# A fp32 two-model transformer forward in one kernel: where weight conversions, table loads and filler matmuls stand in each engine's order

## The chip, the cores and the metric

One core of one Trainium2 chip runs the whole program. The metric is the time of one execution in device microseconds. The engines named here are PE (TensorE, with its weight loads PEld), DVE (VectorE), ACT (ScalarE), POOL (GpSimd) and SP (SyncE, which issues the weight loads).

## The reference

256 tokens, width 1024, everything in fp32. Two models of two layers each follow one another:

```python
x = x + moba_attention(rms_norm(x, norm_mix[0]))        # 8 heads; one block: causal softmax
x = x + squared_relu_mlp(rms_norm(x, norm_mlp[0]))      # relu(x @ up)**2 @ down, 4096 wide
x = x + pool_mixer(rms_norm(x, norm_mix[1]))            # trailing means over 2, 4, 8, 16 tokens
x = x + squared_relu_mlp(rms_norm(x, norm_mlp[1]))
x = rms_norm(x, norm_final)
# second model; post norms on every branch
x = x + rms_norm(mla_mixer(rms_norm(x)))                # latents 384 + 256, 8 heads, rope part 64
x = x + rms_norm(swiglu(rms_norm(x)))                   # silu(h @ gate) * (h @ up) @ down, 2816 wide
k, v = rms_norm(x, kv_src_g) @ w_kv_shared              # 16 heads of 64
x = x + rms_norm(chunked_mixer(rms_norm(x), k, v))      # chunked attention, relative bias
x = x + rms_norm(swiglu(rms_norm(x)))
```

## The kernel before

**Split products.** Every fp32 product is made from three products of rounded parts: hi x hi, hi x lo and lo x hi. A weight is loaded in chunks of 128 x 2048 (1 MB; 176 chunks, four slots `raw`, `whi`, `wlo`). ACT rounds a chunk (`whi`, L669), DVE subtracts (`wlo`, L1082), PE takes it: three matmuls of up to 512 columns (L1916 to L1918), or a wide form with the activations' two parts side by side (L2015, L2018; at an entry tile by tile L2095, L2097). The chunk's slot is free for the next rounding once PE has used it (`w_used`), and free for the next load once DVE has subtracted (`lo_ready`). Activations are split the same way: ACT copies a turned tile out of PSUM (L725), DVE subtracts (L1209); for heads L747 and L1387; for hidden tiles L783 or L829 and L1419.

**Order.** Nothing schedules this program: each engine has a program written by hand, and semaphores tie them. `cursor` counts the chunks that ACT or DVE has converted; `hi_next` and `lo_next` convert the next one, `lo_before(c)` converts up to chunk c, `hi_half` and `lo_half` convert one half of 1024 columns at a time. An instruction that waits holds up all behind it on its engine. Chunks by stage: qkv 0 to 11, output 12 to 15, first MLP 16 to 47, pool 48, second MLP 49 to 80, latents (`wa`, `uqr`, `uq`, `ukv`) 81 to 89, output 90 to 93, first gated layer 94 to 126, shared keys and values (`kvk`, `kvv`) 127 to 134, queries 135 to 138, output 139 to 142, second gated layer 143 to 175.

**Entries of stages.** A post norm (`post_entry`, ACT's `split_stats`) takes the squares by halves of a tile, scales x + y (`xs`, L1255), and PE turns it (L1958) and starts the next layer while the norm's second factor is still open: `sum_entry`, `late_roots` and `ffn_layer` carry it as a diagonal (`probs`, L1169) that PE spreads over a row (L2107) and DVE multiplies into the gates. Two token tiles t = 0, 1 follow one another. In the latent preparation the 384 and 256 wide latents are normed, turned in four parts (`turn_lora`), and multiplied by `uq`, `uqr` and `ukv`. In an attention, heads (or pairs of heads in the second one, `pair_step`) are staggered: scores, exponentials, probabilities, values, output copies (`copy_out` on ACT, `split_out` on DVE), and weight conversions come between (`due`). `keep_busy` runs matmuls on constants whose result nobody reads. `preload(ACT.Sqrt)` makes a table load (L663) at a chosen place. The last norm is `post_stats` on ACT and `post` on DVE, whole tiles of 1024 columns at a time, and SP stores four halves.

## Time and profile before

| | us |
|---|---|
| median of three runs | 1115.6 |
| the runs | 1114.78, 1115.79, 1115.6 |
| the profiled execution | 1115.45 |
| its span in the trace | 1112.9 |
| PE busy in it | 1079.3 |
| first idle: the start, until the first weights and x are there | about 2.5 |
| last matmul's end to the span's end | about 8.3 |

The span is what the profiler saw from the first to the last instruction; the time of the execution holds 2.55 us more around it. In the timeline a row starts with its start in us from the span's start, then the busy time; in brackets stands the idle time before it on its engine and what ended that. Of the matmuls, ends are modelled, so the pause before one counts from a modelled end.

### The profile page before, as it was taken

What the parts mean: (1) busy time and instruction counts of PE and PEld (TensorE: products, weight loads), DVE (VectorE), ACT (ScalarE), POOL (GpSimd) and SP (SyncE); (2) the same over time, 40 slices, a digit from 0 to 9 for tenths busy, and PEclk for the clock granted to TensorE, in tenths of its full rate; (3) what the DMA queues carried; (4) which work ended last, traced back from release to release, by engine and by line L of the source; (5) the groups of instructions that cost most, each with busy time, mean ns of one, the idle gap of its engine ahead of it and who ended that gap; (6) DMA issues with size and microseconds to landing.
All of it is one profiled execution on the core that took longest, in us unless ns stands there. A gap on an engine that the chain in (4) does not pass through costs nothing.

```text
span 1112.9 us, 15305 instructions
## 1 busy us (share of the span) xinstructions
PE 1079.3 (97%) x5820; PEld 911.4 (82%) x5820; DVE 743.5 (67%) x1056; ACT 558.8 (50%) x710; POOL 37.2 (3%) x58
## 2 busy tenths in 40 slices
PE   8999999999999999999999999999999988999997
PEld 6887888888888888889778788888789677888885
DVE  5756665656777565668677776565897867766665
ACT  5556444444454343436474554444654655454452
POOL 1000000000000000000000110000300200000000
PEclk9999999999999999999999999999999999999999
DMA  9943265555555646446432664656476224655641
GB/s 338 328 153 114 95 219 196 179 197 177 163 164 192 218 159 215 162 130 227 152 104 86 211 203 160 219 187 229 132 261 214 56 68 151 212 186 168 211 165 38
DMA packets 127161, 195.81 MB, mean 176 GB/s; under 512 B 6977, under 2 KB 97217, under 8 KB 126994
## 3 DMA queue, kind: packets, MB, share of 16 engines
q1 hardware_dynamic: 123904, 185.77, 50.2%
q0 software_dynamic: 3216, 9.51, 3.0%
q8 instruction: 26, 0.43, 0.2%
q14 instruction: 13, 0.11, 0.0%
q10 hardware_dynamic: 2, 0.00, 0.0%
HBM read 194.21 MB, written 1.05 MB: 175 GB/s over the span
## 4 chain that ended last, share of the span: by engine, by line
PE 83%; DVE 9%; ACT 5%; issue 2%; DMA 0%; DVEq 0%; ACTq 0%
PE ps L2015 22%; PE ps L1916 14%; PE ps L1918 14%; PE ps L1917 14%; PE ps L2018 11%; DVE wlo L1082 3%; ACT whi L669 2%; PE ps L1958 1%; PE ps L2134 1%; PE ps L2493 1%; DVE act L1209 1%; PE ps L2095 1%; DVE arena L1302 1%; PE ps L2491 1%; PE ps L2528 1%
## 5 line engine op out<-in xcount | busy, mean ns | idle before, releaser
L1082 DVE TENSOR_TENSOR wlo<-raw,whi 128x2048 fp32r<-128x2048 f32 (+2 forms) x171 | 386.4, 2276 | 108.6 <-ACT whi L669 108.1
L2015 PE MATMUL ps<-act,whi 128*128 128x512 f32 x1200 | 424.4, 397 | 2.5 <-DVE wlo L1082 2.5
L669 ACT ACTIVATE whi<-raw 128x2048 fp32r<-128x2048 f32 (+2 forms) x172 | 321.3, 1887 | 33.5 <-PE ps L1918 23.0
L2018 PE MATMUL ps<-act,wlo 128*128 128x256 f32 x1200 | 336.6, 281 | 0.0
L2015 PEld LDWEIGHTS ps<-act,whi 128*128 128x128 f32 x1200 | 225.1, 188 | 57.2 <-DVE wlo L1082 2.2
L2018 PEld LDWEIGHTS ps<-act,wlo 128*128 128x128 f32 x1200 | 226.7, 189 | 1.9
L1916 PE MATMUL ps<-whi,hhi 128*128 128x512 f32 x400 | 156.6, 392 | 3.5 <-DVE hlo L1419 3.5
L1918 PE MATMUL ps<-whi,hlo 128*128 128x512 f32 x400 | 157.1, 393 | 0.0
L1917 PE MATMUL ps<-wlo,hhi 128*128 128x512 f32 x400 | 156.6, 392 | 0.0
L1916 PE MATMUL ps<-whi,act 128*128 128x512 f32 (+2 forms) x286 | 112.5, 393 | 3.8 <-DVE act L1387 2.2
L1918 PE MATMUL ps<-whi,act 128*128 128x512 f32 (+2 forms) x286 | 108.0, 378 | 0.0
L1917 PE MATMUL ps<-wlo,act 128*128 128x512 f32 (+2 forms) x286 | 107.6, 376 | 0.0
L1429 DVE TENSOR_TENSOR arena<-ps,arena 128x512 f32<-128x512 f32 x32 | 22.1, 691 | 113.3 <-ACT arena L788 113.3
L1916 PEld LDWEIGHTS ps<-whi,hhi 128*128 128x128 f32 x400 | 75.1, 188 | 21.1 <-issue 4.4
L1918 PEld LDWEIGHTS ps<-whi,hlo 128*128 128x128 f32 x400 | 75.1, 188 | 16.3
L788 ACT ACTIVATE arena<-ps 128x512 f32<-128x512 f32 x32 | 19.1, 597 | 136.9 <-PE ps L2018 135.4
L1917 PEld LDWEIGHTS ps<-wlo,hhi 128*128 128x128 f32 x400 | 75.1, 188 | 14.9
L1916 PEld LDWEIGHTS ps<-whi,act 128*128 128x128 f32 x286 | 53.8, 188 | 14.3 <-DVE act L1387 3.5
L1918 PEld LDWEIGHTS ps<-whi,act 128*128 128x128 f32 x286 | 53.8, 188 | 9.8
L1917 PEld LDWEIGHTS ps<-wlo,act 128*128 128x128 f32 x286 | 54.0, 189 | 7.8
L817 ACT ACTIVATE arena<-ps 128x512 f32<-128x512 f32 x44 | 26.1, 594 | 65.8 <-PE ps L2018 64.2
L1419 DVE TENSOR_TENSOR hlo<-arena,hhi 128x512 fp32r<-128x512 f32 x50 | 34.4, 688 | 22.8 <-ACT hhi L829 21.4
(226 smaller groups left out, 1128.9 us busy)
## 6 DMA issues: line engine op xcount, KB each, us to landing
raw<-mlp_w_up_in SPq DMA_DIRECT2D x32, 1024.0 KB, 6.2
raw<-mlp_w_down_in SPq DMA_DIRECT2D x32, 1024.0 KB, 4.9
raw<-ffn_w_gate_in SPq DMA_DIRECT2D x22, 1024.0 KB, 5.3
raw<-ffn_w_up_in SPq DMA_DIRECT2D x22, 1024.0 KB, 5.4
raw<-ffn_w_down_in SPq DMA_DIRECT2D x22, 1024.0 KB, 4.8
raw<-attn_w_qkv_in SPq DMA_DIRECT2D x10, 1024.0 KB, 8.6
raw<-w_kv_shared_in SPq DMA_DIRECT2D x8, 1024.0 KB, 5.5
raw<-attn_w_o_in SPq DMA_DIRECT2D x4, 1024.0 KB, 5.0
```

What stands on the lines that cost most here:

```text
L669: nc.scalar.activation(whi[:, s, 0:width], raw[:, s, 0:width], ACT.Copy).then_inc(hi_ready, 1)
L788: nc.scalar.activation(by_token(up_sum), wide(b)[1], ACT.Copy).then_inc(f.rest_copied, 1)
L817: nc.scalar.activation(by_token(dst), wide(b)[1], ACT.Copy).then_inc(f.rest_copied, 1)
L1082: nc.vector.tensor_tensor(wlo[:, s, 0:width], raw[:, s, 0:width], whi[:, s, 0:width].bitcast(F32), ALU.subtract).then_inc(lo_ready, 1)
L1209: nc.vector.tensor_tensor(act_quarter(act_lo, name, p), bank(turned_bank(name, p)).rearrange("p (k t) -> p k t", t=P), act_quarter(act_hi, ...
L1419: nc.vector.tensor_tensor(lo[:, :, :].rearrange("p k t -> p (k t)"), hf, hi[:, :, :].rearrange("p k t -> p (k t)").bitcast(F32), ALU.subtr ...
L1429: nc.vector.tensor_tensor(by_token(up_sum), wide(b)[0], by_token(up_sum), ALU.add)\
L1916: nc.tensor.matmul(dst, lhsT=left[0], rhs=right[0], start=start, stop=False, **kw)
L1917: nc.tensor.matmul(dst, lhsT=left[0], rhs=right[1], start=False, stop=False, **kw)
L1918: return nc.tensor.matmul(dst, lhsT=left[1], rhs=right[0], start=False, stop=stop, **kw)
L2015: nc.tensor.matmul(bank(b + f), lhsT=w[0][:, at:at + P], rhs=act[:, k, :, :].rearrange("p a t -> p (a t)"), start=k == 0, stop=False, skip ...
L2018: ins = nc.tensor.matmul(bank(b + f, 0, T), lhsT=w[1][:, at:at + P], rhs=act_hi[:, k, :], start=False, stop=k == KT - 1, skip_group_check= ...
```

## The change

In the order in which the parts stand in time:

- First attention: DVE's fifth copy of queries, keys and values comes without the conversion ahead of it; the two chunks are converted later, between heads. The Sqrt table is loaded two steps of the head loop later.
- MLP layers: the third chunk is converted in two halves, one on either side of the first squared relu.
- Pool entry: ten filler matmuls are taken out; ACT instead of DVE scales the band's second half.
- Second MLP's entry: chunk 50 is converted after the splits of the entry.
- Latent preparation: chunk 87 before the root, 88 before the query split, the query scales after it, both rotary steps together; on PE, `turn_lora` 2 and 3 stand in the middle of `uq`, and the first tile of values ahead of the query turns.
- Latent attention: after head 8 no more conversions; chunk 95 and 96 are converted behind `post_entry`, and the gain on x behind the loop.
- Gated layers: the conversion behind `sum_up(0)` goes behind `scale_gate(0)`. At the end of the first, chunk 127 is rounded before the last gate's function and subtracted by halves; SP loads it ahead of the last two chunks of the layer.
- Second attention: the Sqrt table is loaded one pair later, and one product of the second token tile is kept back until the last wait. Chunk 144 is half converted before the entry of the last layer, with a new semaphore `half_chunk_hi`.
- Last gated layer: the last two down chunks are taken tile by tile (`last_downs`, so far used in the first gated layer only), and the last norm takes its sums by halves (`last_post`).

DVE, entry of the last gated layer, from the last splits of `post_entry` (L1209) on; L1302 and L1306 update x, L1460 is the first sum of a gate. Before:

```order
L1209 TENSOR_TENSOR act<-ps,act 128x4x128 x2
L1082 TENSOR_TENSOR wlo<-raw,whi 128x2048 x2
L1302 TENSOR_TENSOR arena<-ps,rows 128x512 x2
L1306 SCALAR_TENSOR_TENSOR x<-arena,stat,x 128x512 x2
L1460 TENSOR_TENSOR arena<-ps,arena 128x512
```

After, from the last head's split on (L1214 was L1209, L1103 is a half conversion):

```order
L1412 TENSOR_TENSOR act<-ps,act 128x256 x2
L1103 TENSOR_TENSOR wlo<-raw,whi 128x1024
L1235 TENSOR_SCALAR stat<-stat 128x1
...
L1214 TENSOR_TENSOR act<-ps,act 128x4x128 x2
L1103 TENSOR_TENSOR wlo<-raw,whi 128x1024
L1087 TENSOR_TENSOR wlo<-raw,whi 128x2048
L1309 TENSOR_TENSOR arena<-ps,rows 128x512 x2
```

Half a conversion moved from behind the splits to ahead of the statistics.

DVE, a little later in the same layer: the diagonals (`probs`), the first up sum (L1465, L1493 after), the scale row and the first hidden tile's split (L1419, L1445 after). Before:

```order
L1169 TENSOR_SCALAR probs<-const,stat 128x128 x2
L1465 TENSOR_TENSOR arena<-ps,arena 128x512
L1082 TENSOR_TENSOR wlo<-raw,whi 128x2048
L1175 COPY scale_row<-ps 128x256
L1470 TENSOR_TENSOR arena<-arena,scale_row 128x512
L1478 TENSOR_TENSOR arena<-arena 128x512
L1419 TENSOR_TENSOR hlo<-arena,hhi 128x512
```

After:

```order
L1174 TENSOR_SCALAR probs<-const,stat 128x128 x2
L1493 TENSOR_TENSOR arena<-ps,arena 128x512
L1180 COPY scale_row<-ps 128x256
L1498 TENSOR_TENSOR arena<-arena,scale_row 128x512
L1087 TENSOR_TENSOR wlo<-raw,whi 128x2048
L1506 TENSOR_TENSOR arena<-arena 128x512
L1445 TENSOR_TENSOR hlo<-arena,hhi 128x512
```

The conversion went behind the scaling that ACT's function waits for.

DVE, latent preparation: `xs` are the normed latents, the conversion of 1536 columns is chunk 87, L1732 (L1761 after) the split of a turned part. Before:

```order
L1786 TENSOR_SCALAR xs<-xs,stat 128x64
L1789 TENSOR_SCALAR q_scale<-stat 128x2
L1790 TENSOR_SCALAR q_scale<-stat 128x2
L1082 TENSOR_TENSOR wlo<-raw,whi 128x1536
L1732 TENSOR_TENSOR act<-ps,act 128x2x128 x2
```

After:

```order
L1087 TENSOR_TENSOR wlo<-raw,whi 128x1536
L1800 RECIPROCAL stat<-stat 128x4
...
L1816 TENSOR_SCALAR xs<-xs,stat 128x64
L1087 TENSOR_TENSOR wlo<-raw,whi 128x2048
L1761 TENSOR_TENSOR act<-ps,act 128x2x128 x2
L1832 TENSOR_SCALAR q_scale<-stat 128x2
```

One conversion went ahead of the roots, and the next one took its place.

The diff, cut:

```diff
@@ SP, end of the first gated layer
+                if layer == 0:
+                    load_one(AT["kvk"])
                 load_one(n0 + 31)
                 load_one(n0 + 32)
                 if layer == 0:
-                    for c in range(AT["kvk"], AT["ffn1"]):
+                    for c in range(AT["kvk"] + 1, AT["ffn1"]):
                         load_one(c)
@@ ACT
-                    if h == at.heads - 1:
+                    if h == at.heads + 1:
                         preload(ACT.Sqrt)
...
-                if j == KT - 1:
+                if j == KT:
                     preload(ACT.Sqrt)
...
-                split_stats(act, sum_squares, root, post_name, done, acc, (0, 1, 2))
+                split_stats(act, sum_squares, root, post_name, done, acc, (0, 1))
+                if half_done[0]:
+                    hi_half()
+                split_stats(act, sum_squares, root, post_name, done, acc, (2,))
...
                 copy_rest(gate, n0 + 3 * (NF - 1), GATE)
+                if f is ffn[0]:
+                    hi_next()
                 head(NF - 1, False)
...
+            act.wait_ge(scale_ready, 6)
+            nc.scalar.activation(band[:, :, T:3 * P], const_band[:, :, T:3 * P], ACT.Copy,
+                                 scale=norm_stat("mix1", 1, 6)).then_inc(band_second, 1)
...
-                if j < KT - 2:
+                if j < KT - 2 or j == KT:
                     hi_half()
             ffn_layer(ffn[1], "fpre1", "post1", AT["bwo"] + 4, ACC["bwo"])
-            post_stats(act, sum_squares, root, "fpost1", ffn[1].first + 33, ACC["ffn1"])
+            split_stats(act, sum_squares, root, "fpost1", ffn[1].first + 33, ACC["ffn1"], range(4))
+            root("fpost1", 1)
@@ DVE
+                if then == "fpre1":
+                    lo_half(3)
...
-            def post(name, before=None, then=None):
+            def last_post(name, before):
...
                 for t in range(TT):
...
+                    dve.wait_ge(squares, start + 2 * t + 1)
+                    link(nc.vector.tensor_scalar(st(t, 1, 1, 2), st(t, 0, 0, 1), norm_stat(before, t, 4), EPS,
+                                                 ALU.mult, ALU.add))
+                    multiply(t, 0)
+                    dve.wait_ge(squares, start + 2 * t + 2)
+                    nc.vector.scalar_tensor_tensor(out=st(t, 1), in0=st(t, 0, 1, 2), scalar=norm_stat(before, t, 4),
+                                                   in1=st(t, 1, 1, 2), op0=ALU.mult, op1=ALU.add)\
+                        .then_inc(var_ready, 1)
+                    multiply(t, 1)
+                    dve.wait_ge(root_ready, 2 * NORM[name] + t + 1)
...
-                    if h and due(cursor[0], w_o, h - 1):
+                    if 0 < h < converted and due(cursor[0], w_o, h - 1):
                         lo_next()
...
-                while cursor[0] < n0 + 3:
+                while cursor[0] < n0 + 2:
                     lo_next()
+                lo_half()
                 square(0, GATE)
+                lo_half()
...
                 sum_up(0)
-                lo_next()
                 copy_scales(name)
                 scale_gate(0)
+                lo_next()
...
+                if f is ffn[0]:
+                    lo_half()
                 sum_up(NF - 1)
...
-                lo_before(2 * i + 1)
+                if i < 5:
+                    lo_before(2 * i + 1)
...
+                newton(1).then_inc(scale_ready, 2)
                 gained("mix1", 3)
                 release_row()
-                link(newton(1))
-                nc.vector.tensor_scalar(band[:, :, T:3 * P], const_band[:, :, T:3 * P], st(1, 6), None, ALU.mult)\
-                    .then_inc(band_second, 1)
...
-            sum_entry("mlp1", [(pool_part, p + 1) for p in range(3)] + [(w_used, AT["pool"] + 1)],
-                      lambda: lo_before(mlp[0].first + 31))
+            sum_entry("mlp1", [(pool_part, p + 1) for p in range(3)] + [(w_used, AT["pool"] + 1)])
+            lo_before(mlp[0].first + 31)
...
+            lo_before(AT["wa"] + 3)
             dve.wait_ge(root_ready, 2 * NORM["lora"] + 2)
...
-            lo_before(AT["wa"] + 3)
+            lo_before(AT["wa"] + 4)
             split_lora(2)
             split_lora(3)
...
-            attention(mla, lambda h: (chunked[:, P:T], chunked), AT["mwo"], last_heads)
+            attention(mla, lambda h: (chunked[:, P:T], chunked), AT["mwo"], last_heads, mla.heads + 1)
+            premix_x("post0", 1)
+            post_entry("post0")
             lo_before(AT["mwo"] + 2)
-            post_entry("post0")
@@ PE
                     if 0 < k < KT - 2:
-                        head_out(w_o, k - 1, final, (1,))
+                        second_half_out(k - 1, 0)
+                        if k < KT - 3:
+                            second_half_out(k - 1, 1)
...
+                second_half_out(KT - 4, 1)
                 pe.wait_ge(at.o_lo, KT)
...
-                with pe.Fori(2, NF - 1 if then else NF) as i:
+                with pe.Fori(2, NF - 1) as i:
...
-                if then:
-                    gate_up(n0 + 29, NF - 1, n0 + 30)
-                    last_downs(f, n0 + 31, n0 + 32, NF, then, (5, 6))
-                else:
-                    down(n0 + 32, NF - 1, n0 + 33, last=True)
+                gate_up(n0 + 29, NF - 1, n0 + 30)
+                last_downs(f, n0 + 31, n0 + 32, NF, then, (5, 6) if then else ())
...
-            keep_busy(5, 7)
...
+                    if j == 1 and h == 1:
+                        turn_lora(2)
+                        turn_lora(3)
...
             keys_up(0)
+            values_up(0, (0,))
             pe.wait_ge(qr_roped, 1)
```

## Rows read from the trace of the kernel before

**Rows 1.** Page, parts 1 to 3: busy time, PE's clock by slices, the load queue.

```profile
PE 1079.3 (97%) x5820; PEld 911.4 (82%) x5820; DVE 743.5 (67%) x1056; ACT 558.8 (50%) x710; POOL 37.2 (3%) x58
...
PEclk9999999999999999999999999999999999999999
...
q1 hardware_dynamic: 123904, 185.77, 50.2%
```

**Rows 2.** Waits of PE: us in total, times, longest.

```profile
PE ps L1916 <- DVE hlo L1419: 3.5, 3, 1.3
...
PE ps L1916 <- DVE wlo L1082: 2.2, 2, 1.6
```

**Rows 3.** Groups by line: busy us, mean ns, idle us before and what ended it.

```profile
L669 ACT ACTIVATE whi<-raw 128x2048 fp32r<-128x2048 f32 (+2 forms) x172 | 321.3, 1887 | 33.5 <-PE ps L1918 23.0 <-PE ps L2018 6.4 <-DVE raw L1618 3.6
```

**Rows 4.** Timeline, first attention: start, us, engine, line, operation, idle before.

```profile
83.58 0.69 ACT L903 ACTIVATE xs<-ps,stat 128x512 f32<-128x512 f32 x1 [1.37 <-PE ps L1918]
...
84.45 0.74 DVE L1586 TENSOR_SCALAR xs<-ps,stat 128x512 f32<-128x512 f32 x1
...
86.65 0.33 PE L2134 MATMUL ps<-const,probs 128*128 128x128 f32 x1 [1.48 <-DVE probs L1381]
```

**Rows 5.** Timeline, DVE, first hidden tile of the first MLP.

```profile
134.86 0.69 DVE L1419 TENSOR_TENSOR hlo<-arena,hhi 128x512 fp32r<-128x512 f32 x1 [0.70 <-ACT hhi L783]
```

**Rows 6.** Timeline, ACT and PE, pool entry.

```profile
302.48 1.15 ACT L934 ACTIVATE arena<-const,stat 128x1024 f32<-128x1024 f32 x1 [0.94 <-DVE stat L1648]
...
302.82 0.39 PE L1918 MATMUL ps<-whi,last_hlo 128*128 128x512 f32 x1
303.05 2.32 PE L1935 MATMUL ps<-const 128*128 128x256 f32 x10
305.21 1.03 PE L2371 MATMUL ps<-arena,xs 128*128 128x256 f32 x4
```

**Rows 7.** Timeline, PE, entry of the second MLP.

```profile
323.46 0.39 PE L2095 MATMUL ps<-act,whi 128*128 128x256 f32 x1 [1.32 <-DVE act L1209]
```

**Rows 8.** Timeline, PE, latent preparation.

```profile
529.87 0.39 PE L1916 MATMUL ps<-act,whi 128*128 128x256 f32 x1 [1.58 <-DVE wlo L1082]
```

**Rows 9.** Timeline, PE, end of the latent attention.

```profile
588.23 0.50 PE L1916 MATMUL ps<-whi,act 128*128 128x512 f32 x1 [1.31 <-DVE act L1387]
```

**Rows 10.** Timeline, DVE and PE, entry of the first gated layer.

```profile
603.77 2.29 DVE L1082 TENSOR_TENSOR wlo<-raw,whi 128x2048 fp32r<-128x2048 f32 x1 [1.11 <-ACT whi L669]
...
616.51 0.64 PE L2107 MATMUL ps<-probs,const 128*128 128x128 f32 x4
...
624.18 0.47 PE L1916 MATMUL ps<-whi,hhi 128*128 128x512 f32 x1 [1.33 <-DVE hlo L1419]
```

**Rows 11.** Timeline, ACT and DVE, norm at the entry of the shared keys.

```profile
782.56 0.60 ACT L702 ACTIVATE junk<-ps 128x512 f32<-128x512 f32 x1
...
785.07 0.21 DVE L1236 SCALAR_TENSOR_TENSOR stat<-stat 128x1 f32<-128x1 f32 x1
```

**Rows 12.** Timeline, ACT and PE, end of the second attention.

```profile
899.04 1.28 ACT L663 ACT_TABLE_LOAD   x1
900.33 0.20 ACT L663 ACTIVATE table<-const 128x1 f32<-128x1 f32 x1
...
904.97 0.50 PE L1916 MATMUL ps<-whi,act 128*128 128x512 f32 x1 [0.94 <-DVE act L1387]
```

**Rows 13.** Timeline, PE, entry of the last gated layer.

```profile
922.15 0.50 PE L2015 MATMUL ps<-act,whi 128*128 128x512 f32 x1 [0.82 <-DVE wlo L1082]
...
934.69 0.35 PE L2107 MATMUL ps<-probs,const 128*128 128x128 f32 x1 [1.17 <-DVE probs L1169]
```

**Rows 14.** Timeline, ACT and DVE, the last norm.

```profile
1104.69 1.02 ACT L702 ACTIVATE junk<-ps 128x1024 f32<-128x1024 f32 x1 [1.08 <-PE ps L1918]
...
1106.77 0.21 DVE L1119 TENSOR_SCALAR stat<-stat 128x1 f32<-128x1 f32 x1
...
1109.04 1.42 DVE L1322 SCALAR_TENSOR_TENSOR x<-xs,stat,x 128x512 f32<-128x512 f32 x2
```

More of the change, by code:

```diff
@@ L228, in two_blocks @@
         lo_ready = sem("lo_ready")
+        half_hi = sem("half_chunk_hi")
         w_used = sem("w_used")
@@ L541, in norm_stat @@
             return stat[:, what, n:n + 2, 0] if t is BOTH else stat[:, what, n + t, lo:hi]
-        SUMS = {name: 2 if name in ("lora", "mix1") or name in POSTS else 1 for name in NORMS}
+        SUMS = {name: 2 if name in ("lora", "mix1", "fpost1") or name in POSTS else 1 for name in NORMS}
         def squares_before(name):
@@ L1310, in update_x, with st, multiply @@
                     dve.sem_inc(row_used, 2)
-            def post(name, before=None, then=None):
+            def last_post(name, before):
+                start = squares_before(name)
+                def st(t, k, lo=0, hi=1):
+                    return norm_stat(name, t, k, lo, hi)
+                def multiply(t, h):
+                    cols = slice(h * HALF, (h + 1) * HALF)
+                    nc.vector.tensor_tensor(xs[:, t, cols], bank(2 * t + h), row(name)[:, cols], ALU.mult)
                 wait_row(dve, name)
@@ new lines, in last_post @@
+                    link(nc.vector.scalar_tensor_tensor(out=st(t, 5), in0=st(t, 3), scalar=st(t, 1), in1=st(t, 3),
+                                                        op0=ALU.mult, op1=ALU.mult))
+                    link(nc.vector.tensor_scalar(st(t, 5), st(t, 5), -0.5, 1.5, ALU.mult, ALU.add))
+                    link(nc.vector.scalar_tensor_tensor(out=st(t, 6), in0=st(t, 5), scalar=norm_stat(before, t, 6),
+                                                        in1=st(t, 3), op0=ALU.mult, op1=ALU.mult))
@@ L1388, in split_out, with attention @@
                                         ALU.subtract).then_inc(at.o_lo, 1)
-            def attention(at, masks, w_o, fill):
+            def attention(at, masks, w_o, fill, converted=99):
                 for h in range(at.heads + 4):
@@ L2197, in pairs_from, with second_half_out @@
             def pairs_from(at, first, score, value, w_o, final, name, before):
+                def second_half_out(k, half):
+                    col = (k % 2) * D + half * HALF
+                    ins = product(bank(2 + half), acts(k, P, T), cols(slot(w_o + k // 2), col, col + HALF),
+                                  start=k == 0, stop=False, skip_group_check=True)
+                    if k % 2 and half:
+                        ins.then_inc(w_used, 1)
                 for j in range(first, KT + 1):
@@ L2450, in keys_up, with values_up @@
                 ins.then_inc(k_done, 1)
-            def values_up(j):
+            def values_up(j, tiles=range(TT)):
                 c = AT["ukv"] + j
-                for t in range(TT):
+                for t in tiles:
                     for k in range(2):
@@ L2459, in values_up @@
                                       start=k == 0, stop=k == 1)
-                ins.then_inc(w_used, 1)
+                if tiles[-1] == TT - 1:
+                    ins.then_inc(w_used, 1)
             wait_acts("lora", 4)
```

38 lines of the change are left out of this document (11 added, 27 removed).

## The prediction, made before the changed kernel had run

> **What bounds the kernel now.** Read the busy times first [rows 1]: PE is busy 1079.3 of 1112.9 us, DVE 743.5, ACT 558.8. The matmuls set the time and none of them is taken out, so the change can only win from the 33.6 us in which PE does nothing. The granted clock is at its upper level in every slice (nines in the PEclk line of [rows 1]: 2.4 GHz). Second, the waits of PE [rows 2]: the pauses name DVE conversions and splits, never a weight DMA. Third, the group of ACT's weight copies [rows 3]: the idle time before them is put down to PE (23.0 + 6.4 of 33.5 us), which frees a slot late; the copies never wait for a load. So weights arrive in time, and what is late is a small chain of ACT and DVE work at the entry of a stage, queued behind a 2.29 us weight conversion, a 1.28 us table load or a filler that was put ahead of it. Fourth, the timeline around each pause of PE [rows 4 to 13], and the tail behind the last matmul, 1104.7 to 1112.9 [rows 14].
>
> **How a pause is priced.** I move the start of the late operation to the end of what it really needs, and read what PE's next start becomes. The printed pause counts from a modelled end, and the first matmul behind a pause is recorded as 0.50 us [rows 12, 13] where one in a row of them takes 0.39 and the next starts 0.23 after it [rows 6], so a pause that goes whole returns up to 0.15 more than its length. I take that only where the pause goes whole.
>
> **The parts, in order of time.**
>
> *First attention.* DVE's copy starts at 84.45, behind a conversion of 2.29 us, though ACT's twin copy starts at 83.58 [rows 4]. The change drops that conversion from this place: the copy can start 0.87 earlier. PE's pause of 1.48 shrinks to about 0.6. The conversion itself is made up between later heads, where DVE has idle time. Gain **0.85**.
>
> *First MLP, first hidden tile.* PE waits 0.83 of the 3.5 us in [rows 2] for the split at 134.86; DVE itself was idle 0.70 in front of it [rows 5]. The conversion ahead is cut in halves of about 1.15 (half of 2.29) around the square; the second half fills the 0.70 of idle and adds 0.45, the first leaves 1.08 to 1.15 out of the chain. Gain **0.65**; in the other MLP there is no such pause, so nothing.
>
> *Pool entry.* The band is ready on ACT at 302.48 + 1.15 = 303.63, but the pool's matmuls start at 305.21 [rows 6], behind ten fillers that the change removes. Start about 303.75. The second half of the band goes to ACT, after it, about 1.15 plus a wait for the root: ready near 306.9, where PE needs it some 2 us behind its start. Gain **1.45**.
>
> *Second MLP entry.* PE pauses 1.32 for the first tile's split [rows 7], which stands behind a conversion of 2.29 on DVE. With the conversion behind the splits the pause falls to 0.1; PE comes to that chunk only behind the second tile's 32 small matmuls on the chunk before it (some 3.8 us by my estimate, against two splits of 0.64 and the 2.29), and the conversion ends just before. Gain **1.2**.
>
> *Latent preparation.* The pause of 1.58 waits for a conversion of 1536 columns, 1.72 by width [rows 8]; a second one of 0.6 waits for the next (2.2 in two waits [rows 2]). The change makes the first conversion while DVE waits for the roots, and the second ahead of the query splits. Both pauses go: 2.2 + 0.3. The price is that normalising the latents starts some 1.2 later (1.72 less the half us that DVE waits there for a root now); PE has 18 matmuls of 256 columns, half of 0.23 each, 2.1 us, that cover it. A tie at the turned rotary queries costs 0.1. Gain **2.45**. If the cover is short, 1.0 of it comes back.
>
> *End of the latent attention.* The last split of heads stood behind a conversion and a gain that the change puts after it. PE's 1.31 [rows 9] goes whole. Gain **1.45**.
>
> *First gated layer, entry.* Here moving costs something. The conversion that left the attention now stands in front of the one that began at 603.77. That one had waited 1.11 for ACT [rows 10], so 2.29 + 0.15 less 1.11 and what the splits give up is 1.0 of real shift. The diagonals behind it come 1.0 later, and PE, which had no pause at 616.51, gets one of about 1.0. Then the next conversion goes behind the scaling, and the pause of 1.33 at 624.18 [rows 10] goes. The net is 1.33 + 0.15 - 1.0: gain **0.5**. The bounds are 1.5 (no shift) and -0.6 (the shift whole, the pause left).
>
> *Entry of the shared keys.* The variance step at 785.07 could start when the squares of the first tile end, 782.56 + 0.60 + 0.1 = 783.26, but DVE stood in a conversion [rows 11]. That chunk's load is now issued ahead of the layer's last two, ACT copies it ahead of the last gate's function, and DVE converts a half earlier. The chain moves 1.8, PE's turns behind it 1.7. Moving the load costs the two behind it one load each: 1 MB by the queue's row is 3.15 us of all sixteen DMA engines (185.77 MB in 50.2% of 1112.9) [rows 1]. ACT's copies show no wait for loads [rows 3] and the gap of a load to its need is longer than that in this layer, so nothing to 3 us, and I take nothing. Gain **1.7**.
>
> *End of the second attention.* The table load, 1.28 at 899.04, runs ahead of the copy of head pair 6 [rows 12]; it moves one pair later, into idle time, and one product of three matmuls (3 x 0.23 = 0.7) is held back to fill the last wait. Together they take 0.75 of the 0.94 at 904.97. The same preload moves in the first two attentions are worth nothing there. Gain **0.75**.
>
> *Last gated layer.* The first half of the first output chunk is converted ahead of the statistics. The pause at 922.15 goes (0.98 by start times). Behind the splits stand 1.15 + 2.29 instead of 2 x 2.29, so the diagonals come 2.2 earlier in all, and the pause of 1.17 at 934.69 goes too [rows 13]: another 1.2. Then the 1.32 of [rows 2] (the third wait for L1419: 3.5 - 1.33 - 0.83) goes as in the other layer, with 0.15: 1.5. Gain **3.7**.
>
> *Tail.* Before, tile 1's squares of 1.02 start with the last matmul's end at 1104.69, but DVE is still storing tile 0 and takes up the variance only at 1106.77; the last x ends at 1109.04 + 1.42 = 1110.46, 5.77 behind the squares' start [rows 14]. After, tile 0 is complete 18 matmuls before the end, at 0.23 each 4.1 us, enough for its norm. What is left behind the last matmul: half squares 0.60 + 0.2, one variance step 0.2, a half multiply 0.7 with the root hidden in it, four small steps 0.75, two x updates 1.42: 3.87. That is 1.9 to 2.0 less; waiting once for the last split costs 0.15. Gain **1.8**.
>
> **The sum.** 0.85 + 0.65 + 1.45 + 1.2 + 2.45 + 1.45 + 0.5 + 1.7 + 0.75 + 3.7 + 1.8 = 16.5. Where a pause is removed by less than the next dependence allows, two ends fall together; at five such ties (latent queries, first gated entry, shared keys, both diagonals) I take off 0.1 each: 16.0. The profiled execution took 1115.45 us (span 1112.9, 2.55 around it), within 0.15 of the median 1115.6. Forecast 1115.45 - 16.0 = **1099.5**.
>
> **A rule against the table moves.** The rows show a load of 1.28 us that ends at 900.32, and the next ACT operation at 900.33 [rows 12]. The Trainium skill (ScalarE: Activation LUTs, "What ACT_TABLE_LOAD costs") gives the same load and a drain of 1380 ns on top, 2.66 us a switch. The trace shows no such drain here.
>
> **Rivals.**
> *The waits come back.* A conversion taken out of one chain is due in the next. For it: DVE waits for ACT's copy 1.1 us at both gated entries, so both engines are tight there, and part of my gain is lost already at 616.51. Against it: DVE is busy only 67% [rows 1]. If the second MLP's entry, the latent cover and both gated entries each return about half of theirs (0.6 + 1.0 + 0.5 + 1.9), the time is 1115.45 - 12.0 = **1103.5**.
> *The table load blocks the last head.* It now stands right before the copy of the last head in three attentions. Were 1.28 us of it exposed each time, 3.8 of the gain goes: **1103.3**. For it, the copy can't pass the load; against it, ACT is idle for longer than that before the last head's product.
> *The clock falls (slower).* The fillers between the first MLP and the pool are the only matmuls taken out. If PE's pause there let the granted clock drop to 1.2 GHz, each us of matmul work would take two; the gain of 16.0 is gone once 16 us of full-level work run so, and with 20 us the time is **1119.5**. Against it: the clock line shows no dip around pauses of 1.3 to 1.6 us [rows 1, 4, 8, 9].
> *The change does less than it says.* Were the pauses only renamed (another producer late at the same time), only pool entry, latent attention's end and tail stay: 1115.45 - 4.7 = **1110.7**.
>
> **How the numbers follow.** Forecast 0.74, waits back 0.14, table load 0.05, renamed 0.04, clock 0.03. The range takes in the forecast with its open bounds (latent cover 1.0, first gated entry 1.1, the load up to 3 at the shared keys; below, ties that cost nothing and pauses that I left standing, 2) and the two rivals at 1103.4: 1097.5 to 1104. A measurement tells 0.2%, about 2.2 us, from no change. Faster 0.96, same 0.01, slower 0.03.
>
> **What would show it.** In the trace after: no pause of PE over 0.3 at the pool, at the latent preparation, at the end of the latent attention, at both hidden tiles of the gated layers; one new pause of about 1.0 for the diagonals of the first gated layer; PE busy unchanged but for ten fillers (1077); last matmul near 1090.5, and the last x update about 3.9 behind it. Wrong would be: waits for weight DMAs at the end of the first gated layer, pauses for chunks at the entries, a table load in front of a late copy, or a PEclk digit under nine.

## The result and the profile after

| | before | after |
|---|---|---|
| median | 1115.3 us (4 runs, 1114.78 to 1115.79) | 1098.53 us (4 runs, 1098.49 to 1098.98) |
| profiled execution | 1115.45 | 1098.55 |
| its span | 1112.9 | 1096.3 |
| PE busy | 1079.3 | 1077.0 |

The ratio after to before is 0.9848, with a 95% interval of 0.9837 to 0.986. The change takes 16.8 us off; 16.0 were forecast, and the time lies 1.0 us under the forecast and inside the range. The medians of this document leave out two executions, one of latent_dve_back (1518.83 us) and one of the kernel before (1329.78 us), in which the mean granted clock over the whole span was 0.654 and 0.753. Neither the granted clock nor the DMA volume explains the gain, and of PE's busy time only 2.3 us went, with the fillers: of the page after, parts 1 to 3 answer to [rows 1].

```profile
PE 1077.0 (98%) x5810; PEld 909.4 (83%) x5810; DVE 743.1 (68%) x1061; ACT 560.8 (51%) x716; POOL 37.2 (3%) x58
...
PEclk9999999999999999999999999999999999999999
...
q1 hardware_dynamic: 123904, 185.77, 51.0%
```

What went is mostly idle time of PE: 1112.9 - 1079.3 = 33.6 us before, 1096.3 - 1077.0 = 19.3 after. That is 14.3 of the 16.6 us of span; the other 2.3 are the fillers. Its waits after (us in total, times, longest), where [rows 2] had 3.5 us for L1419 and 2.2 us for the conversions in front of L1916; L2135 is the spreading of the diagonals, L2107 before:

```profile
PE ps L2043 <- DVE wlo L1087: 1.8, 3, 1.1
PE ps L2162 <- ACT junk L738: 1.3, 2, 0.7
...
PE ps L2135 <- DVE probs L1174: 1.0, 1, 1.0
...
PE ps L2162 <- DVE probs L1406: 0.8, 2, 0.6
PE ps L2405 <- ACT arena L935: 0.6, 1, 0.6
```

Neither old wait is left. The wait for the diagonals is a new one: before there was one of 1.2 us in the last gated layer and none in the first; now the last layer has none and the first has 1.0. To say where the time came from I match the matmuls of the two traces one by one and read by how much the same matmul starts earlier. On the long dense stretches between the places this lead holds still, and each step from one stretch to the next belongs to one place (the leads are 0.86, 1.57, 2.92, 4.03, 6.65, 8.27, 8.80, 10.57, 11.31 and 15.03, and 16.63 at the span's end):

| part | forecast | measured at its place |
|---|---|---|
| first attention | 0.85 | 0.86 |
| first MLP, halves | 0.65 | 0.71 |
| pool entry | 1.45 | 1.35 |
| second MLP's entry | 1.2 | 1.11 |
| latent preparation | 2.45 | 2.62 |
| end of latent attention | 1.45 | 1.62 |
| first gated entry | 0.5 | 0.53 |
| shared keys' entry | 1.7 | 1.77 |
| second attention | 0.75 | 0.74 |
| last gated entry | 3.7 | 3.72 |
| tail | 1.8 | 1.60 |
| sum | 16.5, less 0.5 for ties | 16.63 |

The starts behind the table are those of PE's matmuls in the timeline after; [rows 4, 6, 9, 10, 13] hold the same matmuls before.

```profile
85.79 0.33 PE L2162 MATMUL ps<-const,probs 128*128 128x128 f32 x1 [0.61 <-DVE probs L1406]
...
302.21 1.10 PE L2405 MATMUL ps<-arena,xs 128*128 128x256 f32 x4 [0.56 <-ACT arena L935]
...
580.09 0.39 PE L1944 MATMUL ps<-whi,act 128*128 128x512 f32 x1
...
609.16 0.35 PE L2135 MATMUL ps<-probs,const 128*128 128x128 f32 x1 [0.99 <-DVE probs L1174]
...
615.48 0.39 PE L1944 MATMUL ps<-whi,hhi 128*128 128x512 f32 x1
...
909.86 0.45 PE L2043 MATMUL ps<-act,whi 128*128 128x512 f32 x1
...
921.17 0.35 PE L2135 MATMUL ps<-probs,const 128*128 128x128 f32 x1
```

The matmul at 580.09 was at 588.23 with 1.31 us of idle before it; now it has none. The one at 609.16 was at 616.51 with none; now it has 0.99. The one at 615.48 was at 624.18 with 1.33; now none. So the first gated entry gave one pause back and took one away, as the prediction had it.

At the shared keys, the variance step of [rows 11] has left the conversion and waits for ACT's squares:

```profile
774.49 0.22 DVE L1241 SCALAR_TENSOR_TENSOR stat<-stat 128x1 f32<-128x1 f32 x1 [0.36 <-ACT junk L698]
```

It stands 10.58 earlier than 785.07, and 8.80 of that were there before this place: 1.8, as forecast. PE's pause of 1.54 before the turns behind it is gone.

The end of the second attention had two pauses before, the 0.94 of [rows 12] and this one:

```profile
901.33 0.52 PE L2134 MATMUL ps<-const,probs 128*128 128x128 f32 x3 [1.06 <-ACT junk L742]
```

After, the 0.94 is gone and the 1.06 is down to 0.67. The prediction put the whole gain on the 0.94; the table load's share of it shows in the other pause.

The tail, ACT and DVE after, against [rows 14]:

```profile
1089.99 0.60 ACT L698 ACTIVATE junk<-ps 128x512 f32<-128x512 f32 x1 [1.37 <-PE ps L1946]
...
1090.71 0.22 DVE L1337 SCALAR_TENSOR_TENSOR stat<-stat 128x1 f32<-128x1 f32 x1 [0.23 <-ACT junk L698]
...
1092.33 1.42 DVE L1350 SCALAR_TENSOR_TENSOR x<-xs,stat,x 128x512 f32<-128x512 f32 x2
```

From the last squares' start to the last x it is 1092.33 + 1.42 - 1089.99 = 3.76, where it was 5.77 and 3.87 were forecast. DVE now stands waiting for ACT's squares (0.23); before, ACT had been done and DVE was still updating x for the first tile. The lead is 15.03 ahead of the last chunks and 14.70 at the last matmul: taking the chunks tile by tile costs 0.33, where 0.15 was forecast, and 1.93 is gained behind the last matmul.

### The profile page after: what moved, and what is told of

Its sections match the earlier page's. It is cut to its first block, busy times and chain, and to the rows that moved or that the text cites. A ratio compares the mean times of both kernels' runs of the same rounds, so it can differ in the third digit from the quotient of the medians.

```text
span 1096.3 us, 15293 instructions
## 1 busy us (share of the span) xinstructions
PE 1077.0 (98%) x5810; PEld 909.4 (83%) x5810; DVE 743.1 (68%) x1061; ACT 560.8 (51%) x716; POOL 37.2 (3%) x58
## 4 chain that ended last, share of the span: by engine, by line
PE 87%; DVE 8%; ACT 3%; issue 1%; DMA 0%; DVEq 0%; ACTq 0%
PE ps L2043 23%; PE ps L1944 15%; PE ps L1946 15%; PE ps L1945 14%; PE ps L2046 12%; DVE wlo L1087 3%; PE ps L2123 1%; PE ps L1986 1%; PE ps L2162 1%; ACT whi L663 1%; DVE act L1214 1%; PE ps L2529 1%; PE ps L2527 1%; PE ps L2188 1%; PE ps L2564 1%
## 5 line engine op out<-in xcount | busy, mean ns | idle before, releaser
L1087 DVE TENSOR_TENSOR wlo<-raw,whi 128x2048 fp32r<-128x2048 f32 (+2 forms) x167 | 377.1, 2274 | 97.4 <-ACT whi L663 97.1
L663 ACT ACTIVATE whi<-raw 128x2048 fp32r<-128x2048 f32 (+2 forms) x171 | 319.4, 1887 | 33.6 <-PE ps L1946 22.7
L1445 DVE TENSOR_TENSOR hlo<-arena,hhi 128x512 fp32r<-128x512 f32 x50 | 34.3, 687 | 21.5 <-ACT hhi L825 21.5
```

The source lines that it names most:

```text
L663: nc.scalar.activation(whi[:, s, 0:width], raw[:, s, 0:width], ACT.Copy).then_inc(hi_ready, 1)
L1087: nc.vector.tensor_tensor(wlo[:, s, 0:width], raw[:, s, 0:width], whi[:, s, 0:width].bitcast(F32), ALU.subtract).then_inc(lo_ready, 1)
L1445: nc.vector.tensor_tensor(lo[:, :, :].rearrange("p k t -> p (k t)"), hf, hi[:, :, :].rearrange("p k t -> p (k t)").bitcast(F32), ALU.subtr ...
```

## The experiments

Twelve kernels ran. Ten start from the changed kernel and undo or add one thing (two_halvings adds two); scale_first_only starts from the kernel before, and pause_filled from latent_dve_back. Their executions differ by up to 3 us in the first 18 us of the program, for a reason that is told under the last heading. I therefore give the span against the changed kernel's 1096.3, less the difference in the start of the hundredth row of PE, and call that the cost.

| kernel | median | span | start later by | cost against the changed kernel |
|---|---|---|---|---|
| mla_end_back | 1099.4 | 1096.4 | -0.2 | +0.3 |
| half_chunk_95 | 1098.02 | 1096.3 | 1.2 | -1.1 |
| conversion_before_scale | 1101.43 | 1099.3 | 0.1 | +2.9 |
| tail_back | 1100.45 | 1100.9 | 3.0 | +1.6 |
| latent_dve_back | 1106.81 | 1104.5 | -0.1 | +8.3 |
| latent_pe_back | 1100.42 | 1098.1 | 0.2 | +1.6 |
| table_loads_back | 1099.19 | 1096.9 | 0.2 | +0.4 |
| load_order_back | 1098.91 | 1096.6 | 0.0 | +0.3 |
| two_halvings | 1096.15 | 1093.8 | 0.0 | -2.5 |
| fillers_back | 1099.7 | 1097.3 | -0.1 | +1.1 |

The kernel before plus one edit, scale_first_only, had a median of 1112.15 and a span of 1109.3; pause_filled is compared with latent_dve_back below.

**Does a conversion moved out of one chain return in the next?** First the two places around chunk 95. The undoing:

```diff
                     premix_x("post0", 0)
+                if h == mla.heads + 2:
+                    premix_x("post0", 1)
-            attention(mla, ..., last_heads, mla.heads + 1)
-            premix_x("post0", 1)
-            post_entry("post0")
+            attention(mla, ..., last_heads)
             lo_before(AT["mwo"] + 2)
+            post_entry("post0")
```

> The changed kernel with one part undone: the latent attention converts after every head again, the second gain on x stands inside its loop, and chunk 95's subtraction stands ahead of the post norm. Theory (a moved conversion is paid for at the next entry): PE's pause of 1.3 us at the attention's end comes back (cost 1.37), but the new pause of 0.99 before the diagonals of the first gated layer goes (gain 1.04), so the kernel is only 0.3 to 0.4 us slower than the changed one, 1098.9. Rival (the two places are independent, the new pause comes from something else): 1.4 slower, 1099.9, with the 0.99 pause still there.

The timeline of PE in mla_end_back:

```profile
581.34 0.50 PE L1945 MATMUL ps<-whi,act 128*128 128x512 f32 x1 [1.31 <-DVE act L1412]
...
609.60 0.35 PE L2136 MATMUL ps<-probs,const 128*128 128x128 f32 x1
```

The pause of 1.31 is back at the attention's end, and the one before the diagonals is gone. By the matched matmuls the first costs 1.6 and the second returns 1.0; some 0.3 of the difference comes back in steps of 0.12 in later layers, so over the whole span the edit cost 0.3. The medians (1099.4 against 1098.53) don't tell the theory from its rival, the trace does: the rival of independent places falls, since the pause of 0.99 is gone. The edit undoes three things at once, though; that chunk 95's 2.29 us are the common cause is settled by the next kernel, which moves this chunk alone.

If so, the conversion belongs in neither. After the change DVE idles twice in the attention's last steps, before the splits of heads 6 and 7:

```profile
577.34 0.42 DVE L1412 TENSOR_TENSOR act<-ps,act 128x256 fp32r<-128x256 f32 x1 [2.03 <-ACT act L743]
...
579.31 0.42 DVE L1412 TENSOR_TENSOR act<-ps,act 128x256 fp32r<-128x256 f32 x1 [1.55 <-ACT act L743]
```

Each holds a half conversion of 1.22, where neither holds a whole one of 2.29. ACT rounds the chunk by halves so that DVE can begin with the first (left out here: a count that a later wait of DVE checks):

```diff
 # ACT, attention
                     if due(cursor[0], w_o, h):
+                        if at is mla and h == at.heads:
+                            hi_half()
                         hi_next()
...
 # DVE, attention
                         lo_next()
+                    if at is mla and h == at.heads:
+                        lo_half(1)
+                    if at is mla and h == at.heads + 1:
+                        lo_half()
```

> The changed kernel, but chunk 95 is rounded and subtracted in two halves inside the latent attention, in the idle times of DVE of 2.03 and 1.55 us before the splits of heads 6 and 7, instead of behind the post norm. Theory: both pauses are gone at once, the one at the attention's end (it stays gone) and the one of 0.99 before the diagonals; 1.0 us faster than the changed kernel, 1097.5. Rival (halves delay the last splits, since ACT's copies of the heads queue behind the halves): PE's pause at the attention's end returns by 0.5 to 1.3 and the gain is 0.5 or nothing, 1098.0 to 1098.8.

Cost -1.1, and no pause at the attention's end or before the diagonals (L2141 here). Its median over four runs, 1098.02, hardly shows it: the runs spread from 1096.94 to 1099.88, and the profiled one lost 1.2 us at the start; two_halvings, below, contains the same edit and shows it in five runs that lie close together.

```profile
609.47 0.30 PE L2141 MATMUL ps<-probs,const 128*128 128x128 f32 x1
```

The second edit in two_halvings uses the same idea at the largest pause that the changed kernel has left, at the shared keys. DVE idles 1.70 us for a sum of keys, then sums, then converts chunk 130, and PE waits for that conversion:

```profile
797.90 0.69 DVE L1868 TENSOR_TENSOR arena<-ps,arena 128x512 f32<-128x512 f32 x1 [1.70 <-ACT arena L1039]
...
800.85 0.50 PE L2043 MATMUL ps<-act,whi 128*128 128x512 f32 x1 [1.14 <-DVE wlo L1087]
```

```diff
             update_x("fpost0", 1)
+            lo_half()
             sum_keys(1)
```

> The changed kernel with chunk 95 in halves inside the latent attention (as in half_chunk_95) and, at the shared keys, half of chunk 130 subtracted in the 1.70 us in which DVE waits for the second sum of keys, where PE pauses 1.14 at 799.70. Theory: the pause before the diagonals (0.99) and this one (1.14) both go; 1.9 to 2.1 us faster than the changed kernel behind the first matmuls, 1096.5. Rival (the half conversion delays the sum of keys and PE then waits for that): only the first, 1097.6.

DVE and PE in two_halvings:

```profile
794.97 1.22 DVE L1105 TENSOR_TENSOR wlo<-raw,whi 128x1024 fp32r<-128x1024 f32 x1
...
796.76 0.69 DVE L1874 TENSOR_TENSOR arena<-ps,arena 128x512 f32<-128x512 f32 x1 [0.57 <-ACT arena L1041]
797.37 1.22 DVE L1105 TENSOR_TENSOR wlo<-raw,whi 128x1024 fp32r<-128x1024 f32 x1
...
798.64 0.50 PE L2050 MATMUL ps<-act,whi 128*128 128x512 f32 x1
```

The sum still waits 0.57 for ACT, so the half before it cost it nothing, and PE's matmul starts 2.21 earlier than in the changed kernel: 1.0 from chunk 95 and 1.2 from this. The median is 1096.15 us in five runs (1095.98 to 1096.34), ratio to before 0.9828, interval 0.9814 to 0.9842. It is the fastest kernel here, 2.4 us under the changed one.

**The conversion in front of the scaling.**

```diff
                 sum_up(0)
+                lo_next()
                 copy_scales(name)
                 scale_gate(0)
-                lo_next()
```

> The changed kernel with the conversion in the gated layers back in front of the scale row's copy and the scaling of the first gate. Theory: the 2.29 us stand again in the chain to the first hidden tile and PE's pauses of 1.3 us at both layers come back, 1.35 + 1.39 = 2.7 us slower than the changed kernel, 1101.2. Rival (the chain is set by ACT's function and its table, the conversion only filled the idle time): less than 0.5 slower.

```profile
616.98 0.48 PE L1944 MATMUL ps<-whi,hhi 128*128 128x512 f32 x1 [1.22 <-DVE hlo L1445]
...
930.58 0.47 PE L1944 MATMUL ps<-whi,hhi 128*128 128x512 f32 x1 [1.23 <-DVE hlo L1445]
```

Both pauses are back, at a cost of 2.9 (1.5 at each of the two matmuls). The same edit the other way round, alone in the kernel before:

> The kernel before with one edit: in the gated layers the conversion goes behind the scaling of the first gate. Theory (the parts are independent): PE's pauses of 1.33 and 1.32 go, 2.7 to 2.9 us faster than before, 1112.6, as its undoing cost in the changed kernel. Rival (the first output chunk's order carries it): under 1.5 faster.

It made 2.9 us by the medians (1112.15 against 1115.04 for the kernel before in the same session; ratio 0.9974, interval 0.9963 to 0.9985), with 1.5 at each of the two matmuls, as forecast. So this part needs none of the others.

**The latent preparation: whose order makes the gain?** Undone on DVE alone, with PE's new order kept:

```diff
             ins.then_inc(var_ready, 2)
-            lo_before(AT["wa"] + 3)
             dve.wait_ge(root_ready, 2 * NORM["lora"] + 2)
...
-            lo_before(AT["wa"] + 4)
+            lo_before(AT["wa"] + 3)
             split_lora(2)
...
             rope_queries(0)
+            lo_before(AT["wa"] + 4)
             rope_queries(1)
```

> The changed kernel with DVE's two conversions in the latent preparation where they were (chunk 87 behind the normed latents, 88 between the two rotary steps), PE's new order kept. Theory (DVE's order makes the gain): the pauses for the conversions come back, 1.6 to 2.5 us slower than the changed kernel, 1100.1 to 1101.0. Rival (PE's order makes the gain, since it puts other matmuls before the wait): under 0.5 slower.

This missed by far: 8.3 us instead of 1.6 to 2.5, three times what the whole part gains. PE and DVE in latent_dve_back:

```profile
525.37 0.39 PE L1944 MATMUL ps<-act,whi 128*128 128x256 f32 x1 [2.12 <-DVE wlo L1087]
...
528.82 0.86 DVE L1761 TENSOR_TENSOR act<-ps,act 128x256 fp32r<-128x256 f32 x2 [3.50 <-ACT arena L977]
...
532.11 2.29 DVE L1087 TENSOR_TENSOR wlo<-raw,whi 128x2048 fp32r<-128x2048 f32 x1
...
534.55 0.35 PE L1944 MATMUL ps<-act,whi 128*128 128x256 f32 x1 [3.96 <-DVE wlo L1087]
```

The two orders cross. PE's new order turns the latents late, in the middle of the second query chunk. DVE's old order has the next weight conversion behind the split of that turn and one rotary step, so DVE idles 3.50 us, then works through all of it, and PE waits 3.96 us for the conversion. Pauses of 6.1 us in all; another 1.5 us is the clock (below), and the rest comes mostly in steps of 0.12 through the later layers. Undone on PE alone:

```diff
                 for h in range(4):
...
-                    if j == 1 and h == 1:
-                        turn_lora(2)
-                        turn_lora(3)
                 ins.then_inc(w_used, 1)
+                if j == 0:
+                    turn_lora(2)
+                    turn_lora(3)
...
             keys_up(0)
-            values_up(0, (0,))
...
-            values_up(0, (1,))
+            values_up(0)
```

> The changed kernel with PE's order in the latent preparation as before: the last two parts of the latents turned before the second query chunk, all values after the query turns; DVE's new order kept. Theory: PE meets the turn before the normed latents are there, which DVE now makes 1.2 us later behind the conversion, and waits; together with the values, 0.8 to 1.5 us slower than the changed kernel, 1099.3 to 1100.0. Rival (PE's order is worth nothing, DVE alone makes the 2.6): within 0.2.

```profile
524.34 0.55 PE L1996 MATMUL ps<-const,xs 128*128 128x128 f32 x3 [0.62 <-DVEq L1818]
```

Cost 1.6, just over the range. PE meets the turns too early, as expected: it pauses 0.62 here and 0.29 at the next turn. So of the 2.62, DVE's new order alone makes about 1.0, PE's adds 1.6, and PE's without DVE's loses over 5 against the kernel before. DVE's order pays without PE's; PE's order only pays on top of DVE's.

**Table loads.**

```diff
-                    if h == at.heads + 1:
+                    if h == at.heads - 1:
                         preload(ACT.Sqrt)
...
-                if j == KT:
+                if j == KT - 1:
                     preload(ACT.Sqrt)
```

> The changed kernel with the table loads of the three attentions one or two steps earlier, as before. Theory: nothing in the first two, and in the third the load of 1.28 us is again ahead of the copy of head pair 6: PE waits for the split, with one product now kept back to cover 0.7 of it, so 0.3 to 0.8 us slower than the changed kernel, 1098.9 to 1099.3. Rival (the load in front of the last head's copy costs a part of its 1.28, or of a longer drain, in each of the three): faster than the changed kernel by 0.5 to 3.8.

Cost 0.4. In the first two attentions no matmul moves by more than 0.15; in the third the pause before the probabilities' turn is 1.04, where it is 0.67 in the changed kernel:

```profile
890.73 0.30 PE L2162 MATMUL ps<-const,probs 128*128 128x128 f32 x1 [1.04 <-ACT junk L738]
```

The rival that a load in front of the last head's copy costs something falls. In the changed kernel the copy behind the load waits 0.18 us for PE, not for the table:

```profile
891.12 1.28 ACT L657 ACT_TABLE_LOAD   x1
892.41 0.20 ACT L657 ACTIVATE table<-const 128x1 f32<-128x1 f32 x1
892.79 0.38 ACT L743 ACTIVATE act<-ps 128x256 fp32r<-128x256 f32 x1 [0.18 <-PE ps L2221]
```

The Trainium skill (ScalarE: Activation LUTs, "What ACT_TABLE_LOAD costs") adds a drain of about 1380 ns to each switch. These rows don't show one: the load takes 1.28 us and the next operation starts 0.01 later.

**Load order.**

```diff
                 if layer == 0:
-                    load_one(AT["kvk"])
                 load_one(n0 + 31)
                 load_one(n0 + 32)
                 if layer == 0:
-                    for c in range(AT["kvk"] + 1, AT["ffn1"]):
+                    for c in range(AT["kvk"], AT["ffn1"]):
                         load_one(c)
```

> The changed kernel, but the first chunk of the shared keys is loaded behind the last two chunks of the first gated layer, as before; the conversions stay in the new order. Theory: the load has time anyway (it would land some 3 to 5 us before ACT's copy), so no difference, 1098.5. Rival (its load and the two others then collide, 3.15 us a chunk, and ACT stands in front of the last gate's function): 1 to 3 us slower, with a pause of PE near 765.

Cost 0.3, and none of it near the loads: PE has no pause between 764 and 766 in either kernel, and ACT rounds the chunk at 763.87 here against 763.26. The difference has grown to that by 0.12 at a time through the whole first gated layer, beginning long before the load. So the load order was not needed for the gain at the shared keys; that leaves the conversions' order, which was not undone by itself.

**Fillers.**

```diff
             pe.wait_ge(masks_loaded, 16)
+            keep_busy(5, 7)
             for t in range(TT):
```

> The changed kernel with the ten filler matmuls between the first MLP and the pool put back; ACT still scales the band. Theory: PE is busy with them for 2.2 us where it now pauses 0.56, so 1.4 to 1.7 us slower than the changed kernel there, 1100.1. Rival (they keep the clock up, and taking them out cost some of it back later): under 0.5 slower, or faster, with the granted clock below 1.00 behind the pool in the changed kernel.

```profile
301.31 2.32 PE L1963 MATMUL ps<-const 128*128 128x256 f32 x10
303.47 0.38 PE L2406 MATMUL ps<-arena,xs 128*128 128x256 f32 x1
```

The pool starts at 303.47 instead of 302.21: 1.3 at its place, 1.1 over the span, a little under the range. The clock reads 1.00 behind the pool with and without them. (They are five matmuls, of which each is recorded as two rows. The text up to the prediction took the ten rows for ten instructions.)

**Tail.** The change's `last_downs` and `last_post` of the last layer are taken back to `down(last=True)` and `post`, and ACT's squares to whole tiles.

> The changed kernel with the last norm and the last two down chunks as before (whole tiles of squares, PE takes chunk by chunk). Theory: 1.7 to 1.8 slower than the changed kernel, 1100.3, all of it behind PE's last matmul: from there to the last x update 5.8 instead of 3.9, with PE ending about 0.2 earlier. Rival (the store of the last rows, not the norm, ends the span): 0.5 or less.

Cost 1.6. The last x update here ends at 1096.98 + 1.42 = 1098.40, which is 5.8 behind PE's last end of 1092.59; in the changed kernel it is 1093.75 - 1089.95 = 3.8.

```profile
1096.98 1.42 DVE L1337 SCALAR_TENSOR_TENSOR x<-xs,stat,x 128x512 f32<-128x512 f32 x2
```

**The clock.** Latent_dve_back showed what the slower rival of the prediction had in mind. Windows of it: length, busy us of PE, PEld, DVE, ACT and POOL, then the granted clock, the DMA share and GB/s.

```profile
530.00:532.00 2.00, 0.59 (x5) 0.39 (x4) 1.97 (x6) 1.93 (x3) 0.00 (x0) 1.00 0.02 6
532.00:534.00 2.00, 0.00 (x0) 0.00 (x0) 1.97 (x2) 0.00 (x0) 0.00 (x0) 1.00 0.00 0
534.00:536.00 2.00, 1.45 (x9) 1.48 (x10) 1.97 (x6) 0.00 (x0) 0.00 (x0) 0.79 0.34 31
536.00:538.00 2.00, 2.00 (x11) 2.00 (x11) 0.52 (x2) 0.00 (x0) 0.00 (x0) 0.50 0.86 342
538.00:540.00 2.00, 2.00 (x13) 1.82 (x12) 0.00 (x0) 0.82 (x2) 0.00 (x0) 0.86 0.37 152
540.00:544.00 4.00, 4.00 (x24) 3.04 (x22) 1.17 (x2) 2.52 (x5) 0.00 (x0) 1.00 0.00 0
```

Behind the pause of 3.96 the clock is at 0.50, the lower level of 1.2 GHz, for some 3 us, and the matched matmuls lose another 1.5 us in it. To tell the pause from the clock, fillers went into the pause of latent_dve_back:

```diff
+            keep_busy(16, 3)
             keys_up(0)
```

> The kernel latent_dve_back (DVE's old order with PE's new one, PE pauses 3.96 us at 530.6 and its clock reads 0.79, 0.50, 0.86 in 534 to 540) with 16 filler matmuls of 0.23 us into a spare bank ahead of the wait. The pause for the chunk stays, filled. Theory (the pause itself lets the clock drop): the granted clock stays 1.00 there and the kernel is 1.2 to 1.5 us faster than latent_dve_back, 1106.1. Rival (the clock falls for another reason, or the slow matmuls are slow for another reason): no difference, 1107.5.

```profile
526.00:528.00 2.00, 0.77 (x4) 0.77 (x5) 1.17 (x1) 0.24 (x1) 0.00 (x0) 0.83 0.00 0
528.00:530.00 2.00, 2.00 (x11) 2.00 (x11) 0.00 (x0) 0.00 (x0) 0.00 (x0) 0.50 0.92 236
530.00:532.00 2.00, 2.00 (x16) 2.00 (x15) 0.00 (x0) 0.48 (x3) 0.00 (x0) 0.81 0.72 287
...
538.00:540.00 2.00, 2.00 (x11) 1.77 (x10) 1.85 (x6) 0.00 (x0) 0.00 (x0) 1.00 0.58 119
540.00:544.00 4.00, 4.00 (x31) 3.86 (x30) 0.00 (x0) 0.22 (x1) 0.00 (x0) 1.00 0.50 203
```

As a time it decides nothing: the median is 1108.88, 2.1 over latent_dve_back, where 1.2 to 1.5 less was expected. Each filler took 0.42 us and not 0.23, since I had again read rows as instructions, so the 16 ran from 533.80 to 540.52, 2.75 us past the chunk. The clock half of the expectation held behind the filled pause: 1.00, and the matmuls that had taken 3.48 us from the chunk's first on (534.55 to 538.03) take 2.34 (540.52 to 542.86). But in this execution the clock fell one pause earlier, behind the 2.12 us, at which it had stayed at 1.00 in latent_dve_back. That a pause of PE precedes the drop is shown; at what length it follows is not, and the same pause did it in one execution and not in another.

## Why the prediction was right

The forecast of 1099.5 stands against 1098.53, and every part lies within 0.2 us of its own estimate; the largest errors, +0.17 at the latent preparation and at the end of its attention and -0.2 in the tail, cancel in part. What carried it was the way of pricing: take the late operation, move its start to the end of what it needs, and read PE's next start.

- **The bound.** PE's busy time changed by its fillers only (1079.3 to 1077.0, as forecast). The other 14.3 of the 16.6 us of span were time in which PE was idle, the tail included. Shown by the page and the matched starts.
- **The first gated entry.** The one place where I forecast a new pause. It was forecast as about 1.0 and is 0.99; mla_end_back and half_chunk_95 together show that chunk 95's place causes it, half_chunk_95 that it can be had without.
- **The ties.** This step was off. I took 0.1 off at five places where two ends fall together (and counted the latent queries twice, once inside their part, whose terms 2.2 + 0.3 - 0.1 give 2.4 and not 2.45); the sum without it, 16.5, is nearer to the 16.63 of the traces. Of the rest of the 1.0 us of error, 0.1 lies in the parts and 0.3 outside the span (the two profiled executions differ by 16.9 and their spans by 16.6).
- **Latent preparation.** Right in size, 2.62 for 2.45, but my picture was of two edits side by side, PE's as a cover for DVE's. Latent_dve_back cost 8.3: PE's order needs DVE's, while latent_pe_back keeps 1.0 of the gain with DVE's alone. The forecast for the whole did not suffer, since the whole was what I traced through.
- **The load order.** Taken at nothing, with a bound of 3. Load_order_back shows nothing at its place.
- **The tables.** The 0.75 of the second attention came as 0.74; table_loads_back puts 0.4 of it to the load, so the rest goes to the product kept back and small shifts. That share was not run by itself. The place was half wrong: the load's share came off the pause of 1.06 at 901.33, which the prediction does not name, and not off the 0.94.
- **The signs.** The list allowed no pause over 0.3 at the pool; 0.56 is left there. The list contradicts its own sum: PE's last matmul ahead of the pool ends at 302.82 + 0.39 = 303.21, so a start at 303.75 is a pause of 0.54.
- **The rivals.** "The waits come back" holds at one place, for 1.0; besides, the wait for chunk 130 at the shared keys went from 0.94 (at 811.41 before) to 1.14. "The table load blocks the last head" falls by table_loads_back. "The clock falls" did not happen in the changed kernel. In other executions it fell behind pauses of 1.74, 2.12 and 3.96 us, longer than any that the changed kernel has once its matmuls have begun (1.14). "Less than it says" falls by the table of parts.
- **Not tried:** first attention, the halves in the first MLP, the second MLP's entry, chunk 127's halves at the shared keys, the product kept back in the second attention and chunk 144's half in the last gated layer were not undone one by one; for them there are the matched starts only, some 7 of the 16.63 us.

## What to carry to other kernels

In an order written by hand, a long job that nobody waits for at once must not stand ahead of a short one that somebody waits for; but it has to stand somewhere, so look for where the same engine idles, and if no gap holds it whole, cut it in halves (2.29 us became twice 1.22, and both pauses went). Trace an edit through to the next entry, since what leaves one chain can arrive in the next, as it did at one place here. And when two engines' orders change together, price and test them together: PE's new order without DVE's cost here three times what the pair gained.

## What the runs showed of the hardware

- **The load of x can come late.** DVE's first step on the second token tile needs it. That step starts at 9.89 in the changed kernel's profile, with no wait for the load; in three of the fourteen profiles it waits, 0.98 us in half_chunk_95, 1.01 in pause_filled and 1.65 in tail_back, where it starts at 11.71:

```profile
11.71 0.69 DVE L1543 TENSOR_TENSOR xs<-x,ps 128x512 f32<-128x512 f32 x1 [1.65 <-DMA x<-x_in]
```

- In that execution the granted clock then fell behind PE's pause of 1.74 us, and the hundredth row of PE came 3.0 us late:

```profile
12.00:14.00 2.00, 1.07 (x6) 0.75 (x7) 2.00 (x3) 0.85 (x2) 0.00 (x0) 0.96 1.05 385
14.00:16.00 2.00, 2.00 (x6) 1.61 (x5) 2.00 (x4) 1.63 (x2) 0.00 (x0) 0.50 1.06 388
16.00:18.00 2.00, 2.00 (x7) 1.51 (x7) 1.59 (x2) 0.00 (x0) 0.00 (x0) 0.68 1.11 353
```

- So two executions of like kernels can differ by 1 to 3 us before the first attention has begun. Differences under that are to be read from matched instructions, not from one time. Whether the spread of the executions without a profile has the same cause is not shown.
- A filler matmul of fp32 operands and 256 columns is recorded as two rows, 0.21 us apart: 16 of them took 6.7 us.
